# A two-block transformer kernel on one core: transposes ahead of the latent attention reordered, memory attention taken head by head

## The reference

```python
u = rmsnorm(x, norm_mix_w) @ w_in                       # 3760 columns
y_ssd = ssd_mixer(u_ssd, ...)                           # state-space part, 1024 columns
y_mla = mla_mixer(u_mla, ...)                           # latent attention, 16 heads, 96 per query and key, 64 per value
x = x + concatenate([y_ssd, y_mla]) @ w_out
h, m = rmsnorm(x, norm_memx_w), rmsnorm(mem, norm_mem_w)
# memory attention: 4 heads of 256, 256 memory rows
q, k, v = h @ wq, m @ wk, m @ wv
p = softmax(q @ k.T * 256 ** -0.5)
x = x + (p @ v) @ wo
x = x + conv_ffn(rmsnorm(x, norm_ffn_w), ...)
return rmsnorm(x, norm_final_w)
```

## Time and profile before

| | |
|---|---|
| median of 3 runs | 1033.71 us (1031.39 to 1038.86) |
| profiled execution, time | 1033.83 us |
| profiled execution, span | 1032.0 us |
| granted TensorE clock, mean | 0.993 |
| PE busy | 983.5 us, 95% of the span |
| DVE, ACT, POOL busy | 616.6, 516.2, 74.2 us |
| DMA | 166 MB, mean 161 GB/s |

### The profile page before, as it was taken

One profiled execution on the slowest core, in us unless ns is written; L12 is line 12 of the kernel. 1 busy time (PEld: TensorE's weight loads), 2 busy tenths in 40 slices (PEclk: granted clock), 3 DMA queues, 4 the chain that ended last, 5 costly groups with the idle time before them and its releaser, 6 DMA issues.

```text
span 1032.0 us, 13394 instructions
## 1 busy us (share of the span) xinstructions
PE 983.5 (95%) x5001; PEld 825.3 (80%) x5001; DVE 616.6 (60%) x761; ACT 516.2 (50%) x736; POOL 74.2 (7%) x100
## 2 busy tenths in 40 slices
PE   6999999999999999999999988999997999999996
PEld 5888888787778888887888777989896778888884
DVE  4555455665765445466677883665544557676765
ACT  6534433565663444446465565425342365555553
POOL 2300000000000000001005270100000000000000
PEclk9999999999999999999999998999999999999999
DMA  8856555442445655563553350234651425555541
GB/s 288 266 192 201 176 190 199 168 151 74 164 155 193 195 173 201 186 221 117 176 172 102 104 189 18 83 123 152 216 187 59 164 82 190 177 184 181 179 146 41
DMA packets 106777, 166.01 MB, mean 161 GB/s; under 512 B 5676, under 2 KB 79692, under 8 KB 106604
## 3 DMA queue, kind: packets, MB, share of 16 engines
q1 hardware_dynamic: 104640, 160.39, 46.5%
q0 software_dynamic: 1936, 5.00, 1.6%
q10 hardware_dynamic: 160, 0.07, 0.0%
HBM read 164.38 MB, written 1.05 MB: 160 GB/s over the span
## 4 chain that ended last, share of the span: by engine, by line
PE 87%; DVE 6%; ACT 4%; issue 1%; DMA 1%; POOL 0%; POOLq 0%; ACTq 0%; SPq 0%; DVEq 0%
PE ps L1759 25%; PE ps L1761 25%; PE ps L1760 25%; PE ps L2057 2%; PE ps L2025 1%; DVE w_lo L1182 1%; ACT w_hi L579 1%; PE ps L1952 1%; PE ps L1959 1%; DVE arena L1612 1%; PE ps L1783 1%; ACT xT_hi L634 1%; PE ps L2029 1%; PE ps L2308 1%; PE ps L2320 1%
## 5 line engine op out<-in xcount | busy, mean ns | idle before, releaser
L1182 DVE TENSOR_TENSOR w_lo<-raw,w_hi 128x2048 fp32r<-128x2048 f32 (+2 forms) x143 | 327.3, 2298 | 172.9 <-ACT w_hi L579 172.7
L1759 PE MATMUL ps<-w_hi,xT_hi 128*128 128x512 f32 (+2 forms) x898 | 350.3, 390 | 12.5 <-DVE w_lo L1188 3.3
L1761 PE MATMUL ps<-w_hi,xT_lo 128*128 128x512 f32 (+2 forms) x898 | 340.9, 380 | 0.0
L1760 PE MATMUL ps<-w_lo,xT_hi 128*128 128x512 f32 (+2 forms) x898 | 340.3, 379 | 0.0
L579 ACT ACTIVATE w_hi<-raw 128x2048 fp32r<-128x2048 f32 (+2 forms) x143 | 269.8, 1898 | 90.4 <-PE ps L1761 71.4
L1759 PEld LDWEIGHTS ps<-w_hi,xT_hi 128*128 128x128 f32 x898 | 169.8, 189 | 47.0 <-issue 11.7
L1761 PEld LDWEIGHTS ps<-w_hi,xT_lo 128*128 128x128 f32 x898 | 169.6, 189 | 32.5
L1760 PEld LDWEIGHTS ps<-w_lo,xT_hi 128*128 128x128 f32 x898 | 170.0, 189 | 30.7 <-issue 1.4
L1759 PE MATMUL ps<-w_hi,hT_hi 128*128 128x512 f32 x232 | 90.9, 392 | 1.8 <-DVE hT_lo L1316 1.8
L1761 PE MATMUL ps<-w_hi,hT_lo 128*128 128x512 f32 x232 | 90.5, 390 | 0.0
L1760 PE MATMUL ps<-w_lo,hT_hi 128*128 128x512 f32 x232 | 90.3, 389 | 0.0
(11 more groups left out here) (273 smaller groups left out, 1027.1 us busy)
## 6 DMA issues: line engine op xcount, KB each, us to landing
raw<-in_ffn_w_gu SPq DMA_DIRECT2D x88, 512.0 KB, 4.8
raw<-in_ffn_w_down SPq DMA_DIRECT2D x44, 512.0 KB, 4.0
raw<-in_w_ffn_up SPq DMA_DIRECT2D x44, 512.0 KB, 5.4
raw<-in_w_in SPq DMA_DIRECT2D x38, 512.0 KB, 4.6
raw<-in_w_out SPq DMA_DIRECT2D x24, 512.0 KB, 4.2
raw<-in_w_ffn_down SPq DMA_DIRECT2D x22, 512.0 KB, 4.3
raw<-in_w_mem_k SPq DMA_DIRECT2D x8, 512.0 KB, 4.0
raw<-in_w_mem_v SPq DMA_DIRECT2D x8, 512.0 KB, 5.0
```

The costliest lines, as they stand in the source:

```text
L1182: TTn(w_lo[HOME[k]][:, 0:n], raw[k % RING][:, 0:n], w_hi[HOME[k]][:, 0:n].bitcast(F32), ALU.subtract).then_inc(resid, 1)
L1759: pe.matmul(out_, lh, rh, start=first, stop=False, **kw)
L1760: pe.matmul(out_, lh, rl, start=False, stop=False, **kw)
L1761: return pe.matmul(out_, ll, rh, start=False, stop=last, **kw)
```

## The change

1. **Order of transposes.** PE turns the key heads first (`turn_heads(j)`, j below 8), then `y_ssd`, then the query heads. The heads use the four banks 0, 1, 2, 7 in turn instead of eight, and the turned `y_ssd` lies in banks 3 to 6. ACT and DVE copy heads first and make `xT_hi` and `xT_lo` of `out_ssd` afterwards. POOL's rotation has other scratch (`rope_tmp`) and doesn't wait for `scaled` any more; the mask-row DMAs do.
2. **Splits and squares.** ACT makes the `kvup` splits after each of the first two query copies, and the squares of `y_ssd` after them. DVE scales `y_ssd` after the first key and value copy and makes one split after the second; the split of `out_ssd` unit 1 goes behind the first row maxima. One add of the `y_ssd` chain (`skip_added`) moves ahead of two `decay_mask`s.
3. **Latent attention.** After `scores(0)` both tiles of `out_ssd(0)` follow. In the loop `scores(gi + 1)` is followed by `turn_probs(gi)`, one tile of `out_ssd(gi + 1)`, `weighted(gi)` and the other tile. The last copy of turned probabilities is shared by DVE (1024 columns) and ACT (512). Six of the eight row tiles of `out_mla` are turned ahead of `weighted(3)`, the last two between the two token tiles of its first unit.
4. **Memory attention.** w_mem_q comes in units of one head (8 row tiles by 256 columns). PE interleaves query product, scores, turning, weighted sum and turning of the output by head, with the last two inside `by_rows("mo", 0)` and `by_rows("mo", 1)`; ACT and DVE have matching orders with splits in between.

The diff, cut:

```diff
 # ACT, queries, keys and values
             for i in range(3):
-                if i:
-                    split(U0["qup"] + i + 2)
-                if i == 1:
+                if i == 2:
...
                     squares("out_ssd")
...
+                if i < 2:
+                    split(U0["kvup"] + i)
...
             attention(0, 4)
+            act.wait_ge(pT_ps, 4)
+            act.activation(prob_T(3)[:, 1024:1536], ps[:, 5, :], ACT.Copy).then_inc(pT3_act, 1)
             norm("out_mla")
 # POOL
             pool.wait_ge(q2_dve, 3)
-            pool.wait_ge(scaled, SCALE_FIRST.index("out_ssd") + 1)
...
-            pool.wait_ge(rope2_done, 1)
+            pool.wait_ge(scaled, SCALE_FIRST.index("out_ssd") + 1)
             pool.dma_start(qT2[QK:QK + 2, :, :].rearrange("p a b -> p (a b)"), mla_rows[0]).then_inc(mask_rows_in, 16)
 # DVE, keys and values
-            scaled_input("out_ssd")
             for s in range(4):
-                if s % 2 == 0:
-                    split(U0["kvup"] + s // 2 + 2)
...
+                if s == 0:
+                    scaled_input("out_ssd")
+                elif s == 1:
+                    split(U0["out_ssd"])
             for j in range(1, 16, 2):
...
-            attention(0, 4)
+            turned("out_ssd", 0, KT)
+            row_max(0)
+            split(U0["out_ssd"] + 1)
+            side_add(0)
+            for gi in range(4):
+                if gi < 3:
+                    row_max(gi + 1)
+                prob_T_out(gi)
+                if gi < 3:
+                    split(U0["out_ssd"] + gi + 2)
+                if gi == 2:
+                    scaled_input("mk")
+                attn_out(gi)
+                if gi < 3:
+                    side_add(gi + 1)
+            split(U0["out_mla"] + 1)
             norm("out_mla")
 # PE, latent attention
+            pe.wait_ge(k_rope_spread, 2)
+            for j in range(8):
+                turn_heads(j)
+            norm("out_ssd")
+            pe.wait_ge(rope2_done, 1)
+            for j in range(8, 16):
+                turn_heads(j)
+
+            pe.wait_ge(mask_rows_in, 32)
+            scores(0)
...
+            out_ssd(0, 0)
+            out_ssd(0, 1)
+            for gi in range(3):
+                scores(gi + 1)
+                turn_probs(gi)
+                out_ssd(gi + 1, 0)
+                weighted(gi)
+                out_ssd(gi + 1, 1)
+            turn_probs(3)
+            pe.wait_ge(o_ready, 3)
+            norm("out_mla", 0, 6)
+            weighted(3)
...
+            xT_there("out_mla", 1)
+            for t in range(TT):
+                if t:
+                    pe.wait_ge(o_ready, 4)
+                    pe.wait_ge(x_ready, 2 * XU.index("out_ssd") + 2)
+                    norm("out_mla", 6, 2)
 # PE, memory attention (mem_weighted waits for pT3_ready, mem_turn_out for o3_ready)
+            mem_q(0)
+            mem_q(1)
+            mem_scores(0)
+            mem_q(2)
+            mem_turn(0)
+            mem_scores(1)
+            mem_weighted(0)
+            mem_q(3)
+            mem_turn(1)
+            mem_scores(2)
+            mem_turn_out(0)
+            mem_weighted(1)
+            mem_scores(3)
+            mem_turn(2)
+            by_rows("mo", 0, lambda: mem_late(2))
+            mem_turn(3)
+            by_rows("mo", 1, lambda: mem_late(3))
+            mem_turn_out(3)
+            by_rows("mo", 2)
+            by_rows("mo", 3)
```

More of the change, by code:

```diff
@@ L1662, in _ @@
                 bc(sm[:, 8, SH:2 * SH], SP_), ALU.mult).then_inc(off_read, 1)
+            dve.wait_ge(off_read, 1)
+            dve.wait_ge(skip_ready, 2)
+            TTn(y_ssd[:, 1, :], y_ssd[:, 1, :], xs_tok[:, 1, :], ALU.add).then_inc(skip_added, 1)
             decay_mask(6)
@@ L2072, in out_ssd @@
                     last.then_inc(unit_used, 1)
-            def attention(first, n):
-                scores(first)
-                for gi in range(first, first + n):
-                    if gi + 1 < first + n:
-                        scores(gi + 1)
-                    side = GROUPS[gi][0] == "mla"
-                    if side:
-                        out_ssd(gi - first, 0)
-                    turn_probs(gi)
-                    if side:
-                        out_ssd(gi - first, 1)
-                    weighted(gi)
             pe.wait_ge(ident_in, 32)
@@ L2415, in _, with mem_q @@
                 norm("mq", 2 * i, 2)
-            turned_result("mq")
-            pe.wait_ge(m_act, 1)
-            pe.wait_ge(m_dve, 1)
-            pe.wait_ge(m3_act, 2)
-            pe.wait_ge(m3_dve, 2)
-            attention(4, 2)
-            pe.wait_ge(o_ready, 6)
-            norm("mo")
-            to_1024("mo")
+            def mem_q(h):
+                k = U0["mq"] + h
+                if h == 2:
+                    pe.wait_ge(m_act, 1)
+                pe.wait_ge(resid, k + 1)
+                for r in range(KT):
+                    if h == 0:
+                        xT_there("mq", r // 2 * 2 + 1)
+                    for j in range(2):
+                        last = product(ps[:, MEM_Q_BANK[h], j * S:j * S + S], wt(k, 256 * r + P * j, P),
+                                       (xT_hi[:, r, :], xT_lo[:, r, :]), r == 0 and j == 0, r == KT - 1,
+                                       skip_group_check=True)
+                last.then_inc(unit_used, 1)
@@ new lines, in mem_scores, with mem_turn @@
+            def mem_scores(h):
+                pe.wait_ge(q3_ready, h + 1)
+                if h:
+                    pe.wait_ge(p3_ready, h)
+                for t in range(TT):
+                    for d in range(2):
+                        last = pe.matmul(ps[:, 2, t * S:t * S + S], qT3[:, 2 * h + d, t * P:t * P + P],
+                                         kT3[:, 2 * h + d, :], start=(d == 0), stop=(d == 1))
+                last.then_inc(sc3_ps, 1)
+            def mem_turn(h):
+                pe.wait_ge(p3_ready, h + 1)
+                if h:
+                    pe.wait_ge(pT3_ready, h)
+                for i in range(4):
+                    last = pe.transpose(ps[:, 3, i * P:i * P + P], prob3[h % 2][:, i * P:i * P + P], ident)
+                last.then_inc(pT3_ps, 1)
@@ new lines, in mem_weighted @@
+            def mem_weighted(h):
+                pe.wait_ge(pT3_ready, h + 1)
+                if h == 0:
+                    pe.wait_ge(m_act, 1)
+                    pe.wait_ge(m_dve, 1)
+                else:
+                    pe.wait_ge(o3_ready, h)
+                for t in range(TT):
+                    for kt in range(TT):
+                        at = (t * TT + kt) * P
+                        last = pe.matmul(ps[:, 0, t * S:t * S + S], probT3[h % 2][:, at:at + P],
+                                         v3[:, kt, h * MEMD:h * MEMD + MEMD], start=(kt == 0), stop=(kt == 1))
+                last.then_inc(o3_ps, 1)
```

251 lines of the change are left out of this document (164 added, 87 removed).

## The result

The changed kernel takes 1019.49 us (median of 4 runs, 1017.64 to 1020.0) against 1034.68 for the kernel before, run beside it. The ratio is 0.9849, with a 95% interval of 0.9826 to 0.9872: faster by 13 to 18 us. Forecast were 1016.0 us and a range of 1011 to 1023. The profiled execution took 1017.64 us with a span of 1015.9 and a mean clock of 0.992, so 16.1 us less span than before.

The account below looks back on a forecast made before the run. PE bounds the kernel with 87% of the chain, so only its idle time and clock loss could be won back. First stretch 9.2 plus memory attention 8.6 gave 17.8 us; 1033.8 - 17.8 = 1016.0 us, range 1011 to 1023.

Parts of the forecast that it names:

- The first term: From the end of the value product to scores(0): key transposes start at 607.0, scores at 617.1; 4.8 us gained.
- rival (B): POOL's rotation is late, its waits bring a third clock fall; 4.2 us more, 1020.2; chance 0.12.
- The cover in the loop: Latent attention: side-product tiles remove the 3.49 us wait, its clock fall and the 1.6 us wait; 6.9 us.
- The wait into `out_mla`: Ahead of the first out_mla product: one merged PE wait of 3.9 us, then a clock fall taken as 2.5 us.
- rival (A): At out_mla: DVE quicker by 1.2 us and no clock fall; 1012.3 us; chance 0.14.
- The memory attention: Interleaving by head there removes six PE waits of 8.9 us, with 0.3 left; net 8.6 us.
- (C): Small waits stay at most handovers by head and in the latent attention loop; 4 us more, 1020; chance 0.11.
- (D): Slower than before: many short waits hold PE at 1.2 GHz after 755 us; 1048 us; chance 0.03.
- idle times up to 2.0 were not: On PE's clock: idle times of 2.8 us and more were followed by a fall, those up to 2.0 not.

Follow-up runs that it names:

- the rotation held back: The changed kernel with one wait put back: POOL starts the rotation only when DVE has scaled y_ssd; 1013.55 us.
- Half of the cover: The changed kernel with one side-product tile, out_ssd(0, 1), moved on PE from ahead of scores(1) to behind it; 1025.4 us, ratio 0.9898.
- the kernel with the memory attention alone: The kernel before up to the end of the latent attention, then the changed memory attention; 1023.56 us, ratio 0.9887 to the kernel before.

## Why the prediction was right in its total, and where it was wrong

**The first term failed**, and the step that failed is the start of POOL's rotation: "The factor, and the key copies that began at 596.58 and took 3.23 us, move with them, so the rotation starts at 603.0". The squares did come 3.2 us later, as taken (593.16, in an execution that is 1.2 us ahead). But the key copies took 1.23 us, not 3.23, because the split that had lain beside them was gone; the old time was carried over without asking what made it. So the rotation began at 599.68, or 600.9 on the scale of the kernel before, and not at 603.0. By the sum the eight scalings, at their old 2.2 us, would have been over by then. As it was they ran beside the rotation and took 9.17 us.

From there "PE begins with key heads of the first two steps, whose copies are long made. So PE starts at 607.0" fails too: the copies of step 1 stand on DVE behind the scalings. The forecast knew of the collision, from 1.29 against 3.33 us, but read it in one direction: DVE holds up POOL. So rival (B) priced the rotation late, and it ended early, at 607.6. In place of 4.8 us gained, 0.4 were lost: 4.05 us of waits for 1.3 forecast (0.5 and 0.8, hidden here), and 2.4 us of clock for none. With the rotation held back the stretch from the first transposes took 616.71 - 606.19 = 10.5 us, against the 10.1 of the forecast (607.0 to 617.1).

The Trainium skill, SBUF — State Buffer (Who interferes with whom), states that between a DVE instruction in a two-port mode and GpSimd the one that issues first takes the shared port pair for its whole instruction and the other blocks, and names the scaling's operation among those that can run in such a mode. The prediction used the half of that rule in which POOL is the loser. The trace agrees with the other half as well: about 1380 ns for a scaling that takes 340 alone.

**The cover in the loop** was right: the wait of 3.49 us, its fall and the wait of 1.6 us are gone; 7.3 us for 6.9. Half of the cover brings the wait and the fall back.

**The wait into `out_mla`** was forecast at 3.9 us and measured at 3.88, put together as said from division, split and two `xT_lo`. The clock fell behind it, so rival (A), no fall, is out; the price was 1.7 us for 2.5. The merged wait is worse than a short one, as argued, and it was avoidable by moving one line.

**The memory attention** was mis-sized to the safe side. All six waits went (none of the 0.3 us left over), at a clock of 1.00, so rivals (C) and (D) are out. The term of 8.6 measured 10.3 when the change was made alone, because the removed waits gave back more than their idle time (what exactly, stays open). With the fall of 1.7 us inside the same stretch that gives 8.6, against the 8.2 of the table.

**The rest** is 1.2 us that the changed kernel was ahead before the change begins: at the first transposes of the second block's input the two profiles already stand at 475.76 and 474.53 us, in code that is alike. In the seven kernels built from the changed one the same point lies between 474.64 and 475.62 us. It is a difference of executions and belongs to no term. So the total of 17.8 against 16.1 holds partly by luck: -5.2 in the first term, +0.4, +2.1 and +1.0 in the others. Rival (B)'s 1020.2 us is nearer to the 1019.49 than the forecast is, by a mechanism that didn't occur.

## What to carry to other kernels

When a wait is dropped so that work can start earlier, list what runs on the other engines in the time it moves into, and price the collision for both: here a rotation that nobody needed for 4 us more cost PE 5 us through DVE. And when a time is taken from an old trace, ask what ran beside it there and whether that still does. Put long work of the engine that ends a wait into the idle time ahead of its last input, not behind it; the same instructions in another order were worth 4 us. Fill a handover with work of PE's own, and price a wait with the clock behind it, as a risk: the same wait didn't always bring a fall.

## What the runs showed of the hardware that was not expected

DVE and POOL went instruction by instruction. Two scalings of DVE and the two products of POOL beside them, in the changed kernel, each on its own row:

```profile
601.10 1.39 DVE L1259 TENSOR_SCALAR xs<-arena,rstd 128x256 f32<-128x256 f32 x1
602.42 1.38 DVE L1259 TENSOR_SCALAR xs<-arena,rstd 128x256 f32<-128x256 f32 x1
```

```profile
600.99 1.35 POOL L1185 TENSOR_TENSOR arena<-arena,trig 128x512 f32<-128x512 f32 x1
602.31 1.34 POOL L1185 TENSOR_TENSOR arena<-arena,trig 128x512 f32<-128x512 f32 x1
```

Each scaling ends 0.1 to 0.2 us behind the POOL instruction beside it, eight of them beside two key copies and six instructions of the rotation. A scaling of 340 ns took as long as its neighbour (680 and 700 ns beside the copies of 610 and 670), while POOL lost next to nothing (1.35 for 1.29 us). So here the engine with the short instructions was slowed most: one of them per instruction of the other. With the rotation held back, POOL met DVE's split instead: it lost some 2 us in one product (3350 ns at most, 1302 in the median), the split 0.6 us (2.92 for 2.28). DVE's copies out of PSUM (L1227 at 605.66, four in 1.65 us) ran at their old speed beside POOL's products.

The second mask-row DMA of 612.55 us landed 4.1 us after its issue, with only copies out of PSUM on DVE beside it, and as late (4.1 us) in the changed kernel, with a split beside it. Before, no split lay beside it either, and the 1 MB load of mem followed it on its queue: that load, to which the prediction gave part of the 4.3 us, accounts for 0.2 us at most.

Of the clock, the runs add to the two falls before: it fell behind every idle time of 2.84 us or more from 600 us on, the longest 3.88 us. It did not behind 1.67, 2.04 and 2.37 us. But it fell behind 1.61 us in the kernel with the memory attention alone, and not behind the same 1.61 us in the kernel before. So the prediction's "idle times up to 2.0 were not" held for its trace alone: behind short waits a fall was rare in these profiles, not excluded. The number of falls also varies between executions of one kernel: of the kernel before, eleven executions beside these runs took 1031.21 us at a mean clock of 0.996 to 1038.42 us at 0.988.

Nor does the length of the wait set the price. By PE's busy time a fall cost 1.6 us behind 3.88 and 2.3 behind 3.87 us (136.11 and 136.80 us busy from `out_mla` to the next layer, 134.53 without a fall), and 3.1 us behind 2.94. TensorE: Matmul & The Clock Gate (The HAM clock gate) of the Trainium skill has the throttled state as the default and sustained activity releasing it, which is why a wait can cost more than its length; here that is up to 3.1 us more.
